# Second expert tile: who compares the keys and who weighs the one-hots of the scatter

## The chip, the cores and the metric

One core of a Trainium2 chip runs the kernel. Its engines are named TensorE (PE, with its weight loads as PEld), VectorE (DVE), ScalarE (ACT), GpSimd (POOL) and SyncE (SP, which only issues transfers here). The metric is the device time of one launch in microseconds (us), the median of the runs; lower is better. Times in the trace are counted from the first instruction of one profiled execution.

## The reference, cut to what matters

The model has three parts that follow each other (a gated MLP with spatial mixing, stick-breaking attention, a convolution and mLSTM mixer). The change lies in the last one, a layer of 16384 experts (PEER) for 256 tokens with 2048 features:

```python
q = (xt @ wq).reshape(-1, 8, 2, 128)                     # 8 heads, two half queries
s = einsum('thpc,hpnc->thpn', q, keys)                   # 128 first and 128 second keys
sv, si = top_k(s, 16)                                    # then the best 16 of the 16 x 16 pairs
eid = first_key * 128 + second_key                       # 128 experts for each token
gate = softmax(top_s)
act = gelu(einsum('thkd,td->thk', take(u, eid), xt))     # 128 dot products for each token
out = einsum('thk,thkd->td', gate * act, take(v, eid))
```

So each token has 128 picks: an expert (a pair of a first and a second key) and a weight, `gate * gelu(dot product)`.

## The kernel before, in words

**Tokens and stages.** The 256 tokens are two tiles of 128 (tile 0 and tile 1), a token for each of the 128 partitions. The expert layer has three stages.

1. *Rows of u.* For each of 256 rows (`r`, 128 for each tile) an indirect transfer gathers one row of `u` for each token of the tile, 1 MB in all, into a ring of buffers. VectorE does the dot product of most rows (`dot_row`); for two slots of the ring GpSimd multiplies (`scale_row`) and ScalarE sums (`sum_row`). Between the rows VectorE chooses the experts of later head groups, ScalarE takes exponentials of the gates (`gate_exponent`, the last at row 182), and the scatter of tile 0 is done, one step about every four rows.
2. *Scatter.* The weights of a token are spread into a 128 x 128 table over its two keys: the table of a token is a product of two one-hot matrices, `onehot_b` (pick k has second key b) transposed times `onehot_a` (pick k has first key a, times the weight of pick k). One **step** does this for 4 tokens (`SCATTER`), so a tile has 32 steps (`SCATTERS`). Steps are counted 0 to 31 within tile 1 in this text. A step is: the one-hots are made on the vector engines, TensorE multiplies (4 products, `scatter`, L1124; in fp32 each is two weight loads and two matmuls in the trace, so 8 of each in a step), and ScalarE copies the 4 tables from PSUM into `wT` in SBUF (`store_one`, L1475).
3. *Values.* 128 chunks: each has the dense product of `wT` with a chunk of the first 1152 columns of `v` (transfers of 576 KB by SyncE, products L1149 and L1155), and two gathered rows of the other 896 columns, weighed by VectorE (`weigh`, L2279; gathers by GpSimd, L716). Then the last layer norm and the output.

**Buffers and order.** Every engine runs its own program in the order in which the code is written, and the engines meet at semaphores. The one-hots have 4 slots (`HOT_SLOTS`): whoever fills the slot of step m waits for `scattered` to show that TensorE is done with step m-4. TensorE writes the tables of a step to one of two halves of PSUM: step m waits in `w_stored` for the store of step m-2. Of the value stage, 4 gathers and 3 dense chunks have buffers of their own and are issued before the scatter of tile 1 (`V_EARLY`); the other buffers lie where the one-hots and the picks lie, so the remaining transfers wait for the scatter's last step (`pool.wait_ge(scattered, TOKENS // SCATTER + 2)`, and the same in `load_v`).

**Between the last row of u and the first step of tile 1.** ScalarE copies the keys of tile 1 out of PSUM (`picks_out("keys1")`, L1209), loads the table of Gelu (`warm_up(ACT.Gelu)`, L1230), takes the Gelu of the dot products (`pick_gelu(1)`, L1461). VectorE multiplies with the gates (`weights(1)`, L2213). TensorE turns the weights so that picks lie on partitions (unit `picks1`, L1110), ScalarE copies them into `picksT[:, 2, ...]`. The keys are in `picksT[:, 0]` (first) and `picksT[:, 1]` (second).

**The one-hots of tile 1 before the change.** VectorE compares both keys of the 4 tokens in one instruction (`plain_one_hots`, L2195, 128 x 1024 numbers). Then the plain one-hot of the first key is weighed in place: token 0 of the step by ScalarE (`weigh_one_hot`, L1485), tokens 1 to 3 by GpSimd (`weigh_one_hots`, L703, 128 x 384). TensorE waits for both. ScalarE's order is: weigh step m, store step m-2. In tile 0 (`static_one_hots`) VectorE makes both itself: L2180 compares the second keys (128 x 512), L2184 makes a weighed one-hot of one token (128 x 128) four times.

Of the kernel before, what the change touches and what calls it, by code (L numbers as in the profile page):

```python
# [74 lines left out]
SCATTER = 4  # L75
SCATTERS = P // SCATTER
HOT_SLOTS = 4
ACT_TOKENS = 1

RAW_SLOTS = 4  # L80
SPLIT_SLOTS = 4
# [11 lines left out]
CHOICE_STEPS = (0, 3, 5, 7, 9, 11, 14, 17, 21)  # L93
EXPONENT, FINISH = 5, 8
LAST_ROW = TILES * PICKS - 1


def row_slot(r):
# [112 lines left out]
def build(nc, x, norm_g, a_w_in, a_v_norm_g, a_w_s, a_b_s, a_w_out, b_w_in, b_w_out, final_g, ln_in_g_2, ln_in_b_2,  # L211
# [6 lines left out]
    with ctx:  # L218
# [202 lines left out]
        def sem(name):  # L421
            return ctx.enter_context(nc.semaphore(name))
# [63 lines left out]
        wgt_done = sem("wgt_done")  # L486
        onehot_done = sem("onehot_done")
        weighed_by_pool = sem("weighed_by_pool")
        weighed_by_act = sem("weighed_by_act")
        scattered = sem("scattered")  # L490
        w_stored = sem("w_stored")
        v_raw_landed = [sem(f"v_raw_landed{s}") for s in range(V_CHUNKS)]
# [112 lines left out]
        def _(pool):  # L605
# [90 lines left out]
            def weigh_one_hots():  # L696

                is_emptied(pool, "picks1")
                for m in range(SCATTERS, TILES * SCATTERS):
                    first, end = m * SCATTER + ACT_TOKENS, (m + 1) * SCATTER  # L700
                    cut = onehot_a[m % HOT_SLOTS][:, ACT_TOKENS:, :]
                    pool.wait_ge(onehot_done, m + 1)
                    nc.gpsimd.tensor_tensor(  # L703
                        cut, cut, picksT[:, 2, first:end].unsqueeze(2).to_broadcast([P, SCATTER - ACT_TOKENS, N_KEYS]),
                        ALU.mult).then_inc(weighed_by_pool, 1)

            pool.wait_ge(keys_known, TILES)
            for t in range(TILES):
# [25 lines left out]
        def _(pe):  # L734
# [378 lines left out]
            def scatter(t):  # L1113

                for m in range(t * SCATTERS, (t + 1) * SCATTERS):
                    if t:
                        pe.wait_ge(weighed_by_pool, m - SCATTERS + 1)
                        pe.wait_ge(weighed_by_act, m - SCATTERS + 1)
                    else:
                        pe.wait_ge(onehot_done, m + 1)  # L1120
                    pe.wait_ge(w_stored, m + 1)
                    s = m % HOT_SLOTS
                    for n in range(SCATTER):
                        last = mm(by_128[B][:, m % 2 * SCATTER + n, :], onehot_b[s][:, n, :], onehot_a[s][:, n, :],  # L1124
                                  start=True, stop=True)
                    last.then_inc(scattered, 1)
# [48 lines left out]
        def _(act):  # L1175
# [300 lines left out]
                   by_128[B][:, s * SCATTER:(s + 1) * SCATTER, :].rearrange("p n a -> p a n"), ACT.Copy)\  # L1476
                    .then_inc(w_stored, 1)

            def weigh_one_hot(m):

                act.wait_ge(onehot_done, m + 1)
                for n in range(ACT_TOKENS):
                    token = m * SCATTER + n
                    cut = onehot_a[m % HOT_SLOTS][:, n, :]
                    ins = fn(cut, cut, ACT.Copy, scale=picksT[:, 2, token:token + 1])  # L1485
                ins.then_inc(weighed_by_act, 1)

            act.sem_inc(w_stored, 2)

            for n in range(CHOSEN_BEFORE):  # L1490
# [1 line left out]
            for r in range(TILES * PICKS):  # L1492
                if r == PICKS:
                    pick_gelu(0)
                    weigh_h(0)
                if r == PICKS + 5:
                    picks_out("picks0", picksT[:, :, 0:P], 3)
                if r + 1 == TILES * PICKS:
                    warm_up(ACT.Gelu)
                if by_pool(r):  # L1500
                    sum_row(r)
                for n in range(CHOSEN_BEFORE, ALL_GROUPS):
                    if r == CHOICE_ROW[n] + CHOICE_STEPS[EXPONENT] + 1:
                        gate_exponent(n)
                if r == PICKS - 4:
                    act.wait_ge(gates_done, CHOSEN_EARLY + 1)
                    fn(flat[A], h[:, 1, :], ACT.Copy).then_inc(h_copied, 1)
                for m in range(SCATTERS):
                    if r == one_hot_row(m) + 2:
                        store_one(0, m, m % 2)  # L1510
                if r == one_hot_row(SCATTERS - 1) + 2:
                    picks_out("keys1", picksT[:, 0:2, P:], 2)
            pick_gelu(1)
            picks_out("picks1", picksT[:, 2:3, P:], 1)
            is_emptied(act, "picks1")
            for m in range(SCATTERS + 2):
                if m < SCATTERS:
                    weigh_one_hot(SCATTERS + m)
                if m >= 2:
                    store_one(1, m - 2, m % 2)  # L1520
                if m == 2:
                    weigh_h(1)

            def round_chunk(c):
# [29 lines left out]
        def _(dve):  # L1554
# [632 lines left out]
                                                 op0=ALU.is_equal, op1=ALU.mult)  # L2187
                ins.then_inc(onehot_done, 1)

            def plain_one_hots(m):  # L2190

                wide = [P, 2, SCATTER, N_KEYS]
                token = m * SCATTER
                dve.wait_ge(scattered, m - 1)
                v.tensor_tensor(onehots[:, m % HOT_SLOTS, :, :, :],  # L2195
                                near_keys[1].unsqueeze(1).unsqueeze(1).to_broadcast(wide),
                                picksT[:, 0:2, token:token + SCATTER].unsqueeze(3).to_broadcast(wide), ALU.is_equal)\
                    .then_inc(onehot_done, 1)

            def dot_row(r):  # L2200

# [66 lines left out]
                        static_one_hots(m)  # L2268
            weights(1)
            is_emptied(dve, "keys1")  # L2270

            def weigh(r):

# [9 lines left out]
            def subtract_chunk(c):  # L2283
# [6 lines left out]
                v.tensor_tensor(v_split[u][:, 1, :], v_raw[c % V_CHUNKS][:, 0:V_SPLIT],  # L2290
                                v_split[u][:, 0, :].bitcast(F32), ALU.subtract).then_inc(v_lo, 1)

            for m in range(SCATTERS, TILES * SCATTERS):
                plain_one_hots(m)

            dve.wait_ge(h_weighed, TILES)
            def kept_stats(t):
# [61 lines left out]
```

## Time and profile before

| | |
|---|---|
| runs | 2971.75 us median of 3 (2969.94 to 2973.08) |
| profiled execution: span from first to last instruction | 2967.1 us, 28922 instructions |
| the rest of a run's time around that span (median less span) | 4.6 us |
| PE / DVE / ACT / POOL busy | 78% / 69% / 38% / 28% |
| mean granted TensorE clock | 0.884 of full speed |
| rows of u, both tiles | about 1760 to 2426 us |
| scatter of tile 1 | about 2426 to 2466 us |
| values | about 2466 to 2948 us, then the norm and output to 2967 |

The span is what the trace shows; the time of a run is a little longer since it holds what lies around the instructions. The granted clock of 1.0 is TensorE's level of 2.4 GHz, and 0.5 is that of 1.2 GHz. A row that is merged (x27) gives the time from the first start to the last end.

### The profile page before, as it was taken

Reading aid. Unit: us, or ns where it says so; the run is one execution under the profiler, and the core shown is the slowest. Engines: PE = TensorE matmul, PEld = TensorE weight load, DVE = VectorE, ACT = ScalarE, POOL = GpSimd, SP = SyncE. Lnnn points to the kernel's source line nnn. Section 1 sums busy time; section 2 is a strip of 40 time slices with the busy share of each in tenths; the row PEclk is TensorE's granted clock in tenths of the full one; section 3 lists DMA queues with packets and bytes.
Section 4 is the critical chain, followed back from the end, with each engine's and each line's share of the span. In section 5 each row is a group of like instructions: output and inputs, shape, how many; then the busy total and the mean of one; then the engine's idle time right before and its main releaser. Section 6 shows DMA issues by size and latency. Waiting matters only on the chain.

```text
span 2967.1 us, 28922 instructions
## 1 busy us (share of the span) xinstructions
PE 2323.2 (78%) x10371; PEld 1832.5 (62%) x10371; DVE 2035.6 (69%) x2513; ACT 1129.5 (38%) x1263; POOL 818.3 (28%) x646
## 2 busy tenths in 40 slices
PE   8999999999999999899999990000022249998997
PEld 7888888888888888688888770000011136555654
DVE  5456555554544555745665678999899888887888
ACT  5444344444444554444344442121222244222222
POOL 1000000000000000000000017888787875545553
PEclk9999999999999999999999995555555569999998
DMA  8666556666666546465566569999999977999997
GB/s 281 208 186 193 168 178 191 183 193 190 183 189 184 156 140 207 146 183 177 163 185 227 162 209 395 420 420 418 415 406 400 421 287 291 408 407 390 408 408 301
DMA packets 165303, 792.12 MB, mean 267 GB/s; under 512 B 20188, under 2 KB 20240, under 8 KB 131248
## 3 DMA queue, kind: packets, MB, share of 16 engines
q1 hardware_dynamic: 105344, 390.12, 41.1%
q0 software_dynamic: 59824, 400.23, 33.3%
q8 instruction: 82, 1.34, 0.2%
q14 instruction: 53, 0.43, 0.0%
HBM read 788.17 MB, written 2.10 MB: 266 GB/s over the span
## 4 chain that ended last, share of the span: by engine, by line
PE 57%; DVE 19%; DMA 13%; issue 6%; POOL 3%; ACT 1%; POOLq 0%; DVEq 0%; ACTq 0%
PE banks L749 52%; DMA v_rows<-in_peer_v_rest,eid 11%; DVE ring L2205 9%; DVE banks L2279 3%; DMA ring<-in_peer_u,eid 2%; POOL ring L674 2%; PE banks L781 1%; PE banks L1124 1%; POOL v_rows L716 1%; DVE onehots L2184 1%; DVE v_split L2290 1%; PE banks L761 1%; DVE w_split L1565 0%; DVE cand L2108 0%; PE banks L829 0%
## 5 line engine op out<-in xcount | busy, mean ns | idle before, releaser
L749 PE MATMUL banks<-w_split,xT 128*128 128x512 f32 x7008 | 1611.8, 391 | 8.5 <-DVE xT L1612 5.3
L749 PEld LDWEIGHTS banks<-w_split,xT 128*128 128x128 f32 x7008 | 1314.3, 188 | 282.5 <-DVE xT L1612 6.9
L1565 DVE TENSOR_TENSOR w_split<-w_raw,w_split 128x1024 fp32r<-128x1024 f32 x592 | 722.3, 1225 | 730.6 <-ACT w_split L1187 729.5
L1187 ACT ACTIVATE w_split<-w_raw 128x1024 fp32r<-128x1024 f32 x592 | 626.2, 1059 | 911.6 <-PE banks L749 875.4
L2205 DVE CUSTOM_DVE_ANT_0 ring<-ring,banks 128x2048 f32<-128x2048 f32 x194 | 438.5, 2285 | 46.3 <-DMA ring<-in_peer_u,eid 42.4
L2279 DVE SCALAR_TENSOR_TENSOR banks<-v_rows,wgt,banks 128x896 f32<-128x896 f32 x254 | 293.2, 1154 | 67.6 <-DMA v_rows<-in_peer_v_rest,eid 66.4
L674 POOL DMA_INDIRECT ring<-in_peer_u,eid x256 | 244.8, 956 | 258.4 <-DVE eid L2137 157.8
L716 POOL DMA_INDIRECT v_rows<-in_peer_v_rest,eid x256 | 245.3, 958 | 233.6 <-DVE banks L2279 202.0
L1155 PE MATMUL banks<-v_raw,wT 128*128 128x512 f32 (+1 forms) x1024 | 298.0, 434 | 0.7 <-ACT wT L1475 0.7
L609 POOL DMA_DIRECT2D row_a<-in_final_g x1 | 0.5, 534 | 1067.3 <-DVE ao L1827 1067.3
L1124 PE MATMUL banks<-onehots 128*128 128x128 f32 x512 | 103.0, 367 | 243.7 <-DVE onehots L2184 232.4
L683 POOL TENSOR_TENSOR ring<-ring,h 128x2048 f32<-128x2048 f32 x62 | 280.2, 4520 | 37.7 <-DMA ring<-in_peer_u,eid 36.2
L1448 ACT ACTIVATE ring<-ring 128x2048 f32<-128x2048 f32 x62 | 118.4, 1910 | 403.5 <-POOL ring L683 403.5
L1155 PEld LDWEIGHTS banks<-v_raw,wT 128*128 128x128 f32 x1024 | 174.2, 190 | 134.9 <-issue 123.0
L1110 PE MATMUL banks<-ident,pick_keys 128*128 128x128 f32 x4 | 1.3, 426 | 325.0 <-DVE wgt L2213 325.0
L1124 PEld LDWEIGHTS banks<-onehots 128*128 128x128 f32 x512 | 89.6, 265 | 257.3 <-DVE onehots L2184 241.6
L1149 PE MATMUL banks<-v_split,w_x 128*128 128x512 f32 x768 | 224.5, 423 | 9.6 <-DVE w_x L2287 9.6
L1110 PEld LDWEIGHTS banks<-ident,pick_keys 128*128 128x128 f32 x4 | 0.7, 218 | 325.2 <-issue 325.2
L1149 PEld LDWEIGHTS banks<-v_split,w_x 128*128 128x128 f32 x768 | 122.9, 190 | 58.9 <-DVE v_split L2290 25.0
L1529 ACT ACTIVATE w_x<-wT 128x256 fp32r<-128x256 f32 x128 | 53.2, 416 | 271.4 <-PE banks L1149 271.3
L1531 ACT ACTIVATE v_split<-v_raw 128x512 fp32r<-128x512 f32 x128 | 80.5, 629 | 66.6 <-DMA v_raw<-in_peer_v_dense 65.0
L609 POOL DMA_DIRECT2D row_a<-in_ln_g x1 | 0.5, 528 | 338.4 <-DVE xT L1612 338.4
(321 smaller groups left out, 1320.9 us busy)
## 6 DMA issues: line engine op xcount, KB each, us to landing
w_raw<-in_a_w_in SPq DMA_DIRECT2D x192, 512.0 KB, 3.5
v_raw<-in_peer_v_dense SPq DMA_DIRECT2D x128, 576.0 KB, 8.0
w_raw<-in_b_w_in SPq DMA_DIRECT2D x128, 512.0 KB, 3.5
w_raw<-in_w_in SPq DMA_DIRECT2D x112, 512.0 KB, 3.6
w_raw<-in_a_w_out SPq DMA_DIRECT2D x64, 512.0 KB, 4.5
w_raw<-in_b_w_out SPq DMA_DIRECT2D x32, 512.0 KB, 4.5
w_raw<-in_w_out SPq DMA_DIRECT2D x32, 512.0 KB, 4.4
w_raw<-in_peer_wq SPq DMA_DIRECT2D x32, 512.0 KB, 3.7
```

The lines of the kernel that those rows point to most:

```text
L674: nc.gpsimd.indirect_dma_start(out=ring[s][:, :], out_offset=None, in_=peer_u_2[0], in_offset=bass.IndirectOffsetOnAxis(ap=eid[:, r:r + 1] ...
L683: nc.gpsimd.tensor_tensor(ring[s][:, :], ring[s][:, :], h[:, r // PICKS, :], ALU.mult)\
L716: nc.gpsimd.indirect_dma_start(out=v_rows[r % V_SLOTS][:, :], out_offset=None, in_=peer_v_rest[0], in_offset=bass.IndirectOffsetOnAxis(ap= ...
L749: last = mm(ps[half][:, 2 * t + n, :], xt[:, xp, kk, tok], w_split[:, s, wp, n * BANK:(n + 1) * BANK], start=(k == 0 and xp == 0 and wp == ...
L1124: last = mm(by_128[B][:, m % 2 * SCATTER + n, :], onehot_b[s][:, n, :], onehot_a[s][:, n, :], start=True, stop=True)
L1149: return mm(v_banks[t][0], w_x[u][:, wp, 1 - t, :], v_split[u][:, vp, :], start=first and wp + vp == 0, stop=last and vp == 1)
L1155: mm(v_banks[t][1 + n][:, 0:width], wT[:, 1 - t, c, :], v_raw[s][:, lo:lo + width], start=first, stop=last)
L1187: fn(w_split[:, k % SPLIT_SLOTS, 0, :], w_raw[:, k % RAW_SLOTS, :], ACT.Copy).then_inc(hi_done, 1)
L1448: fn(ring[s][:, :], ring[s][:, :], ACT.Copy, accum_out=wgt[:, r:r + 1]).then_inc(rows_summed, 1)
L1565: v.tensor_tensor(w_split[:, s, 1, :], w_raw[:, k % RAW_SLOTS, :], w_split[:, s, 0, :].bitcast(F32), ALU.subtract).then_inc(split_done, 1)
L2205: v.tensor_tensor_reduce(out=ring[s][:, :], in0=ring[s][:, :], in1=flat[1 - r // PICKS], scale=1.0, scalar=0.0, op0=ALU.mult, op1=ALU.add, ...
L2279: v.scalar_tensor_tensor(out=v_sum, in0=v_rows[r % V_SLOTS][:, :], scalar=wgt[:, r:r + 1], in1=v_sum if m else h[:, t, V_DENSE:], op0=ALU. ...
```

## The change

The one-hots of tile 1 are made in another way. VectorE compares only the second keys (`key_one_hots`, 128 x 512) and makes the weighed one-hot of token 0 (`weighed_one_hots`, 128 x 128). GpSimd makes the weighed one-hots of tokens 1 to 3 from the keys and weights itself, with one `tensor_scalar` each (compare `iota_keys` with the first key, times the weight); it no longer waits for VectorE but for a free slot. ScalarE only stores. TensorE waits for `onehot_done` (VectorE) and `weighed_by_pool` (GpSimd). The second-key one-hots of steps 0 and 1 (`HOT_AHEAD`) are made before the weights are turned. The Gelu table of tile 1 is loaded at row index 183, behind the last exponential, and no longer at row 255.

```diff
-ACT_TOKENS = 1
+DVE_TOKENS = 1
+HOT_AHEAD = 2
+LAST_EXPONENT = CHOICE_ROW[ALL_GROUPS - 1] + CHOICE_STEPS[EXPONENT]
@@ GpSimd
                 is_emptied(pool, "picks1")
+                is_emptied(pool, "keys1")
                 for m in range(SCATTERS, TILES * SCATTERS):
-                    first, end = m * SCATTER + ACT_TOKENS, (m + 1) * SCATTER
-                    cut = onehot_a[m % HOT_SLOTS][:, ACT_TOKENS:, :]
-                    pool.wait_ge(onehot_done, m + 1)
-                    nc.gpsimd.tensor_tensor(
-                        cut, cut, picksT[:, 2, first:end].unsqueeze(2).to_broadcast([P, SCATTER - ACT_TOKENS, N_KEYS]),
-                        ALU.mult).then_inc(weighed_by_pool, 1)
+                    pool.wait_ge(scattered, m - 1)
+                    for n in range(DVE_TOKENS, SCATTER):
+                        token = m * SCATTER + n
+                        ins = nc.gpsimd.tensor_scalar(onehot_a[m % HOT_SLOTS][:, n, :], iota_keys[:, :],
+                                                      picksT[:, 0, token:token + 1], picksT[:, 2, token:token + 1],
+                                                      ALU.is_equal, ALU.mult)
+                    ins.then_inc(weighed_by_pool, 1)
@@ TensorE
                     if t:
                         pe.wait_ge(weighed_by_pool, m - SCATTERS + 1)
-                        pe.wait_ge(weighed_by_act, m - SCATTERS + 1)
-                    else:
-                        pe.wait_ge(onehot_done, m + 1)
+                    pe.wait_ge(onehot_done, m + 1)
@@ ScalarE
-                if r + 1 == TILES * PICKS:
+                if r == LAST_EXPONENT + 2:
                     warm_up(ACT.Gelu)
...
-            for m in range(SCATTERS + 2):
-                if m < SCATTERS:
-                    weigh_one_hot(SCATTERS + m)
-                if m >= 2:
-                    store_one(1, m - 2, m % 2)
-                if m == 2:
+            for m in range(SCATTERS):
+                store_one(1, m, m % 2)
+                if m == 0:
                     weigh_h(1)
@@ VectorE
-            def plain_one_hots(m):
...
+            def key_one_hots(m):
+
                 dve.wait_ge(scattered, m - 1)
...
+                return v.tensor_tensor(onehot_b[m % HOT_SLOTS], near_keys[1].unsqueeze(1).to_broadcast([P, SCATTER, N_KEYS]),
+                                       picksT[:, 1, m * SCATTER:(m + 1) * SCATTER].unsqueeze(2)
+                                       .to_broadcast([P, SCATTER, N_KEYS]), ALU.is_equal)
+
+            def weighed_one_hots(m):
+
+                for n in range(DVE_TOKENS):
+                    token = m * SCATTER + n
+                    ins = v.scalar_tensor_tensor(out=onehot_a[m % HOT_SLOTS][:, n, :], in0=near_keys[1],
+                                                 scalar=picksT[:, 0, token:token + 1],
+                                                 in1=picksT[:, 2, token:token + 1].to_broadcast([P, N_KEYS]),
+                                                 op0=ALU.is_equal, op1=ALU.mult)
+                return ins
@@
             is_emptied(dve, "keys1")
+            for m in range(SCATTERS, SCATTERS + HOT_AHEAD):
+                key_one_hots(m)
...
+            is_emptied(dve, "picks1")
             for m in range(SCATTERS, TILES * SCATTERS):
-                plain_one_hots(m)
+                if m >= SCATTERS + HOT_AHEAD:
+                    key_one_hots(m)
+                weighed_one_hots(m).then_inc(onehot_done, 1)
```

ScalarE's order before, from the copy of tile 1's keys on (`half_free` and `half_filled` are the semaphores of the PSUM halves, `h` the residual rows that are scaled for the value stage):

```order
L1209 ACTIVATE picksT<-banks 128x2x128 [waits half_filled_b]
L1230 ACT_TABLE_LOAD
L1230 ACTIVATE warm<-ident 128x1
L1461 ACTIVATE wgt<-wgt 128x128 [waits rows_summed,rows_used]
L1209 ACTIVATE picksT<-banks 128x128 [waits half_filled_a]
L1485 ACTIVATE onehots<-onehots,picksT 128x128 [waits onehot_done,half_free_a]
L1485 ACTIVATE onehots<-onehots,picksT 128x128 [waits onehot_done] x2
L1475 ACTIVATE wT<-banks 128x128x4 [waits scattered]
L1465 ACTIVATE h<-h 128x896
L1485 ACTIVATE onehots<-onehots,picksT 128x128 [waits onehot_done]
L1475 ACTIVATE wT<-banks 128x128x4 [waits scattered]
```

And now at the same place:

```order
L1210 ACTIVATE picksT<-banks 128x2x128 [waits half_filled_b]
L1462 ACTIVATE wgt<-wgt 128x128 [waits rows_summed,rows_used]
L1210 ACTIVATE picksT<-banks 128x128 [waits half_filled_a]
L1476 ACTIVATE wT<-banks 128x128x4 [waits scattered,half_free_a]
L1466 ACTIVATE h<-h 128x896
L1476 ACTIVATE wT<-banks 128x128x4 [waits scattered] x31
```

The table load and its warm-up have gone from here, and so have the weighings between the stores. The load now stands in the rows of u of tile 1, behind the last exponential (`gate`):

```order
L1449 ACTIVATE ring_154,wgt<-ring_154 128x2048 [waits rows_scaled]
L1455 ACTIVATE gate<-gate 128x32 [waits gate_sub]
L1476 ACTIVATE wT<-banks 128x128x4 [waits scattered]
L1231 ACT_TABLE_LOAD
L1231 ACTIVATE warm<-ident 128x1
L1449 ACTIVATE ring_158,wgt<-ring_158 128x2048 [waits rows_scaled]
```

It lies between a store of tile 0 and the next sum of a row. GpSimd's order before, from its last row of u (`ring`) on:

```order
L683 TENSOR_TENSOR ring_154<-ring_154,h 128x2048 [waits row_landed3]
L716 DMA v_rows_170<-in_peer_v_rest,eid 128x896 [waits keys_known,v_used]
L716 DMA v_rows_171<-in_peer_v_rest,eid 128x896 [waits v_used]
L716 DMA v_rows_172<-in_peer_v_rest,eid 128x896 [waits v_used]
L716 DMA v_rows_173<-in_peer_v_rest,eid 128x896 [waits v_used]
L703 TENSOR_TENSOR onehots<-onehots,picksT 128x384 [waits onehot_done,half_free_a]
L703 TENSOR_TENSOR onehots<-onehots,picksT 128x384 [waits onehot_done] x31
```

And now, from the fourth gather of the value stage on:

```order
L719 DMA v_rows_173<-in_peer_v_rest,eid 128x896 [waits v_used]
L705 TENSOR_SCALAR onehots<-iota_keys,picksT 128x128 [waits scattered,half_free_b,half_free_a]
L705 TENSOR_SCALAR onehots<-iota_keys,picksT 128x128 x2
L705 TENSOR_SCALAR onehots<-iota_keys,picksT 128x128 [waits scattered]
L705 TENSOR_SCALAR onehots<-iota_keys,picksT 128x128 x2
```

One instruction of 128 x 384 a step has become three of 128 x 128, and the wait is for the slot. VectorE now, from its last dot product (`ISA`) on:

```order
L2201 ISA wgt 128x1
L2209 TENSOR_TENSOR wgt<-wgt,gate 128x128 [waits gelu_done]
L2182 TENSOR_TENSOR onehots<-banks,picksT 128x512 [waits scattered,half_free_b,wgt_done]
L2182 TENSOR_TENSOR onehots<-banks,picksT 128x512 [waits scattered]
L2190 SCALAR_TENSOR_TENSOR onehots<-banks,picksT 128x128 [waits half_free_a]
L2190 SCALAR_TENSOR_TENSOR onehots<-banks,picksT 128x128
L2182 TENSOR_TENSOR onehots<-banks,picksT 128x512 [waits scattered]
L2190 SCALAR_TENSOR_TENSOR onehots<-banks,picksT 128x128
```

Where 32 comparisons of 128 x 1024 stood (L2195), two comparisons of 128 x 512 come ahead of the weights, and then one comparison and one weighed one-hot alternate.

## Rows read from the trace of the kernel before

**Rows 1.** Windows: busy us (and instructions) of each engine, TensorE's clock, DMA share, GB/s.
```profile
core 0: us, PE busy (x) PEld busy (x) DVE busy (x) ACT busy (x) POOL busy (x), PEclk, DMA share, GB/s
2168.00:2405.00 237.00, 51.90 (x200) 44.53 (x200) 218.25 (x334) 59.86 (x72) 191.38 (x116) 0.50 1.00 413
2426.00:2466.00 40.00, 37.09 (x257) 32.76 (x257) 36.69 (x33) 29.89 (x68) 27.07 (x33) 0.91 0.09 32
2480.00:2600.00 120.00, 120.00 (x460) 73.29 (x459) 101.43 (x130) 34.54 (x66) 61.69 (x65) 1.00 1.02 408
```

**Rows 2.** Chain of waits into the scatter: start, length, engine, tile, line.
```profile
2424.13 0.37 ACT picksT L1209
2424.52 1.28 ACT L1230
2426.02 0.21 ACT wgt L1461
2426.25 0.30 DVE wgt L2213
2426.58 1.24 DVE onehots L2195
2427.95 0.84 POOL onehots L703
2428.83 11.77 PE banks L1124 x80
```

**Rows 3.** Timeline (start, length, engine, line, ..., idle before): VectorE, GpSimd, ScalarE around the start.
```profile
2424.30 0.08 DVE L2205 DVE_READ_ACCUMULATOR2_ANT wgt<- 128x1 f32 x1
2425.67 0.95 POOL L716 DMA_INDIRECT v_rows<-in_peer_v_rest,eid  x1 [0.30 <-issue]
2427.11 0.28 ACT L1209 ACTIVATE picksT<-banks 128x128 f32<-128x128 f32 x1 [0.89 <-PE banks L1110]
2432.65 30.65 DVE L2195 TENSOR_TENSOR onehots<-banks,picksT 128x1024 f32<-128x1024 f32 x27 [0.32 <-PE banks L1124]
```

**Rows 4.** Timeline: stores of steps 2 to 5 and 31, last step's weight loads.
```profile
2433.79 0.60 ACT L1475 ACTIVATE wT<-banks 128x512 f32<-128x512 f32 x1 [0.25 <-PE banks L1124]
2434.68 0.60 ACT L1475 ACTIVATE wT<-banks 128x512 f32<-128x512 f32 x1
2435.70 0.60 ACT L1475 ACTIVATE wT<-banks 128x512 f32<-128x512 f32 x1
2436.59 0.60 ACT L1475 ACTIVATE wT<-banks 128x512 f32<-128x512 f32 x1
...
2464.33 0.97 PEld L1124 LDWEIGHTS banks<-onehots 128*128 128x128 f32 x8 [0.16 <-POOL onehots L703]
2465.53 0.60 ACT L1475 ACTIVATE wT<-banks 128x512 f32<-128x512 f32 x1 [0.54 <-PE banks L1124]
```

**Rows 5.** Windows of TensorE alone: length, busy (instructions), clock, DMA share.
```profile
2428.80:2433.00 4.20, 4.17 (x19) 0.50 0.23 96
2434.00:2438.00 4.00, 4.00 (x36) 1.00 0.02 4
```

**Rows 6.** Timeline: one-hots of a step of tile 0 on VectorE, GpSimd beside it.
```profile
2406.95 0.69 DVE L2180 TENSOR_TENSOR onehots<-banks,picksT 128x512 f32<-128x512 f32 x1
2407.25 4.52 POOL L683 TENSOR_TENSOR ring<-ring,h 128x2048 f32<-128x2048 f32 x1 [0.58 <-DMA ring<-in_peer_u,eid]
2407.55 1.12 DVE L2184 SCALAR_TENSOR_TENSOR onehots<-banks,picksT 128x128 f32<-128x128 f32 x4
```

**Rows 7.** Groups of GpSimd by form: busy us, mean ns of one.
```profile
L703 POOL TENSOR_TENSOR onehots<-onehots,picksT 128x384 f32<-128x384 f32 x32 | 26.5, 827 | 11.1 <-DVE onehots L2195 11.1
L729 POOL TENSOR_TENSOR h<-h,row_g 128x1024 f32<-128x1024 f32 x1 | 2.4, 2350 | 14.0 <-ACT h L1550 14.0
L616 POOL TENSOR_SCALAR_AFFINE_SELECT upto<-upto 128x128 f32<-128x128 f32 x1 | 0.3, 292 | 0.1
L615 POOL MEMSET upto<- 128x128 f32 x1 | 0.2, 196 | 0.0
```

**Rows 8.** Timeline: ScalarE behind the last exponential of the gates.
```profile
2243.06 0.60 ACT L1475 ACTIVATE wT<-banks 128x512 f32<-128x512 f32 x1 [1.58 <-PE banks L1124]
2246.80 1.91 ACT L1448 ACTIVATE ring<-ring 128x2048 f32<-128x2048 f32 x1 [3.14 <-POOL ring L683]
```

More of the change, by code:

```diff
@@ L488, in build @@
         weighed_by_pool = sem("weighed_by_pool")
-        weighed_by_act = sem("weighed_by_act")
         scattered = sem("scattered")
@@ L1477, in store_one @@
                     .then_inc(w_stored, 1)
[L1479 to L1486, printed above, removed]
             act.sem_inc(w_stored, 2)
@@ L2188, in static_one_hots @@
                 ins.then_inc(onehot_done, 1)
-            def plain_one_hots(m):
-                wide = [P, 2, SCATTER, N_KEYS]
-                token = m * SCATTER
+            def key_one_hots(m):
                 dve.wait_ge(scattered, m - 1)
[L2195 to L2198, printed above, removed]
+                return v.tensor_tensor(onehot_b[m % HOT_SLOTS], near_keys[1].unsqueeze(1).to_broadcast([P, SCATTER, N_KEYS]),
[9 more added lines that the diff above has]
+                return ins
             def dot_row(r):
```

## The prediction

> **What bounds the kernel now.** I read the windows by stage first [rows 1], then the chain of waits through the scatter of tile 1 [rows 2], then the timeline around its start and inside it [rows 3 to 5].
>
> The windows show three stages. While rows of u are gathered, the DMA share is 1.00 at 413 GB/s; in the value stage it is 1.02 at 408 GB/s. Between them lie 40 us, 2426 to 2466, with a DMA share of 0.09 [rows 1]. That hole is the scatter of tile 1: nearly every further transfer needs buffers that the scatter gives back at its end. The value stage is set by transfers, and these start when the last step is done. So I take every microsecond that the scatter ends sooner as one microsecond of the kernel, and nothing that happens to VectorE, GpSimd or ScalarE inside the hole matters otherwise.
>
> Inside the hole VectorE runs 27 comparisons of 128x1024 in 30.65 us without a gap, 1.135 us each, while TensorE waits 0.16 us for GpSimd in each late step [rows 3, 4]. TensorE is busy on paper (37.1 of 40 us), but it waits for one-hots: the bound of the steady part is VectorE's comparison.
>
> Which wait is next if the one-hots come faster? Here the early steps tell. The first ones pile up because TensorE runs at clock 0.50 (1.2 GHz) from 2428.8 to 2433.0, 19 instructions in 4.2 us, and has one-hots waiting when the clock is at 1.00 (2.4 GHz), where it starts about 35 in 4 us [rows 5]. (The granted clock rose 4.2 us after the products began.) In that stretch the stores of steps 2, 4 and of steps 3, 5 stand 1.91 us apart: 2433.79 and 2435.70, 2434.68 and 2436.59 [rows 4]. That is a loop through the two halves of PSUM. Step m may start when step m-2 is stored; from the start of its weight loads to its store are 1.20 us (2464.33 to 2465.53), the store takes 0.60, and the remaining 0.11 is the way from the store's end back to TensorE. 1.20 + 0.60 + 0.11 = 1.91 us for two steps, **0.955 us a step**. ScalarE's weighing is not in the loop as long as it ends before the step is ready to store. TensorE's own rate would be a little quicker than this loop: 8 instructions at 4.0/35 us are 0.91 us.
>
> **The change part by part.** The profiled execution has a span of 2967.1 us; 4.6 us lie around it in the median run of 2971.75. I work out differences in the profiled execution and take them off the median.
>
> *VectorE.* Instead of 1.135 us a step it has one 128x512 comparison and one weighed one-hot. In tile 0 the comparison starts 0.60 us before the next instruction, and four weighed one-hots of 0.34 take 1.12, so one starts each 0.26 us [rows 6]. 0.60 + 0.26 = 0.86 us a step, below 0.955. They keep these durations in tile 0 while GpSimd runs a 4.52 us multiplication beside them [rows 6], so I charge nothing for GpSimd now running at the same time. Two comparisons (1.2 us) are made ahead, while the weights are turned. VectorE is no bound any more.
>
> *ScalarE.* It loses the weighing and keeps 0.60 a step. Free.
>
> *GpSimd.* This is the unknown: three `tensor_scalar` of 128x128 with two scalars from memory; the trace has no such instruction. Bounds from the nearest rows: a memset of 128x128, which reads nothing, takes 0.196 us; a row that reads one tensor and selects by a comparison (affine select, 128x128) takes 0.292 [rows 7]. From above: two-input multiplications take 2.350 us for 1024 and 4.52 for 2048 columns, 2.12 ns a column with 0.18 us to begin with [rows 6, 7], which makes 0.45 us for 128. So a step costs GpSimd 3 x 0.196 = 0.59 to 3 x 0.45 = 1.35 us. I take the affine select, since it too has one input and one output and more than one operation per element, and add a little for the scalars: 0.30 each, **0.90 us a step**, below 0.955. That the same work on 384 columns with two inputs is 0.827 supports it. GpSimd also starts early enough: it can run up to four steps ahead and TensorE loses time to the clock in the first steps.
>
> The Trainium skill has a rule against this choice, in the page GPSIMD Engine Reference, section 7 (performance pitfalls for Q7 kernels): each small read command costs about 102 cycles that do not overlap with the one before. If each of the two scalars were such a read, that would be 0.17 us more at the 1.2 GHz which the page gives, an estimate of 0.46 us an instruction, 1.39 us a step. No row here shows it; the third rival below is what would happen then.
>
> *The start.* Now: the copy of the keys ends at 2424.50, then table load 1.28 and warm-up 0.2, Gelu from 2425.93, weights 2426.25 to 2426.55, turned, copied 2427.11 to 2427.39; VectorE compares from 2426.58 and GpSimd weighs 2427.95 to 2428.79; TensorE starts at 2428.83 [rows 2, 3]. Without the load the Gelu can start when VectorE's last dot product is in, 2424.38, so at 2424.45, 1.5 us earlier; the weights are in `picksT` at 2425.9. VectorE is done with step 0 by 2425.0 + 1.2 + 0.3 = 2426.6. GpSimd, however, is issuing its four gathers of v until 2426.62 [rows 3], which stand ahead of its one-hots. So it starts at 2426.65 and is done with step 0 0.9 us later: TensorE starts at **2427.55 instead of 2428.83, 1.28 us** sooner. Of the 1.5 us of the table load only about 0.8 can be used (without the load moved, GpSimd would start at 2427.45), the rest of the 1.28 is the comparison that GpSimd no longer waits for.
>
> *The table load at row 183.* ScalarE is idle 3.14 us there: the store ends at 2243.66, the next sum starts at 2246.80 [rows 8]. 1.28 + 0.20 fit in. What follows on ScalarE until the Gelu are copies. Cost 0; if the cover were missing, up to 1.5 us for a ring slot that comes free later.
>
> *The steps.* TensorE's step 4 began at 2434.39 + 0.11 = 2434.50, 5.67 us after its start; I keep these 5.67 (clock 0.50 for 4.2 us, then the loop). Step 31 began at 2464.33 [rows 4]: 27 steps in 29.83 us. By the loop they take 27 x 0.955 = 25.78. **4.05 us.** The last step and the store behind it stay the same.
>
> Sum: 1.28 + 4.05 = 5.3 us. GpSimd's limit, checked: its step 31 would be ready at 2426.65 + 32 x 0.90 = 2455.5, TensorE comes to that step at 2427.55 + 5.67 + 25.78 = 2459.0. So an instruction of GpSimd may take up to about (2459.0 - 2426.65)/96 = 0.337 us before it costs anything. Predicted: 2971.75 - 5.3 = **2966.4 us**.
>
> **The rivals.**
> (1) *The loop is not what limits.* If the 1.91 us were ScalarE's order of weighing and storing (0.40 + 0.60 is 1.0 a step, near the 0.955), TensorE would run by itself at about 0.90, the steps would gain 1.4 more: 6.7 in all, 2965.0. Against: the store of step 2 had 0.25 us of idle before it, released by TensorE. An earlier rise of the clock would give as much: each us at 1.00 instead of 0.50 spares about 0.45 us.
> (2) *GpSimd becomes the bound, mildly.* At 0.337 to 0.39 us an instruction the stage ends with GpSimd: at 0.37, step 31 ready at 2426.65 + 96 x 0.37 = 2462.2 instead of the 2464.25 of now; gain 2.1, 2969.7. For it: reading two scalars a time and three starts instead of one. Against: the affine select's 0.292.
> (3) *GpSimd is slower than the comparison it replaced.* The price of three short instructions against one long one; the place is `weighed_by_pool` in front of every product; it decides from (2464.25 - 2426.65)/96 = 0.392 us. At the upper bound of 0.45 step 31 is ready at 2469.9, 5.6 later than now: 2977.4. VectorE and ScalarE would then idle beside it.
> (4) *The gain doesn't reach the end*, because the value stage is bound elsewhere than by transfers. DMA share 1.02 speaks against it. 2971.
>
> **How the numbers follow.** Forecast (the loop, gain 4.5 to 5.9) 0.45; rival 1 0.17; rival 2 0.17; rival 3 0.16; rival 4 0.05. What a measurement can tell from no change is 0.2%, 5.9 us, and the forecast lies just inside of it: 2965.8 is the border. With about 1 us of scatter in a median, the forecast gives faster with 0.38, rival 1 with 0.85, none of the others: 0.17 + 0.14, and some 0.02 for a GpSimd or a clock better than I allow: 0.33. Slower by over 5.9 us needs 0.453 us an instruction, the far end of rival 3: 0.06. Same 0.61. The range goes from 2964.3 (rival 1 with scatter) up to 2973.5 (rival 3 up to 0.41 us an instruction); the forecast's own is 2965.2 to 2967.6.
>
> **What would show it.** In the changed profile: the GpSimd group of `tensor_scalar`, 96 of them, at about 0.30 us (the number on which all hangs); stores of the second tile 0.95 to 0.96 us apart from step 4 on, each second pair 1.91; TensorE's first product at 2427.5; Gelu at 2424.5; the last store 5.3 us earlier; DMA share 1.0 from there and the end as many us earlier; ScalarE's table load in a gap near 2244. Stores 0.90 apart speak for rival 1, a TensorE that waits for `onehots` of GpSimd in each step for rival 2 or 3. The prediction is wrong in its mechanism if the one-hots of VectorE get longer beside GpSimd, or if the value stage takes longer than the 482 us from 2466 to 2948.

## The result, and the profile after

The changed kernel takes 3010.6 us (median of 4, 3006.03 to 3013.05) against 2971.28 us before (4 runs): ratio 1.0127, 95% interval 1.0115 to 1.0139. It is 39.3 us slower; 5.3 us faster was forecast. The profiled execution has a span of 3011.3 us, 44.2 more than the 2967.1 of before; 4.4 of them arise before the scatter (the last dot product ends at 2428.80, before at 2424.38 [rows 3]), as executions differ by some microseconds here.

The group of new GpSimd instructions settles the matter (trace after, instructions that write or read `onehots`, ns min/median/max):

```profile
L705 POOL TENSOR_SCALAR onehots<-iota_keys,picksT x96: 780/781/810, 2431.1 to 2504.6; 128x128 f32<-128x128 f32 x96
L2182 DVE TENSOR_TENSOR onehots<-banks,picksT x32: 675/690/692, 2429.5 to 2497.3; 128x512 f32<-128x512 f32 x32
L2190 DVE SCALAR_TENSOR_TENSOR onehots<-banks,picksT x32: 336/340/343, 2430.7 to 2498.0; 128x128 f32<-128x128 f32 x32
```

0.781 us instead of the 0.30 that I took, and instead of at most 0.45. VectorE's two instructions are as predicted. The chain of waits after, from the gathers of v to the first value products (start, length, engine, tile, line):

```profile
2430.09 0.95 POOL v_rows L719
2431.04 0.05 issue
2431.09 74.30 POOL onehots L705 x96
2505.39 0.04 issue
2505.43 2.09 PE banks L1125 x8
2507.52 0.02 issue
2507.55 0.60 ACT wT L1476
2508.15 0.04 issue
2508.20 4.63 PE banks L1156 x8
```

Where seven kinds of work alternated before [rows 2], one engine's queue is the whole scatter: 96 instructions in 74.30 us, 0.774 from start to start, 2.32 us a step. The waits say the same from the other side (engine line <- who; us, times, longest):

```profile
ACT wT L1476 <- PE banks L1125: 57.9, 32, 5.4
DVE onehots L2182 <- PE banks L1125: 38.7, 28, 2.6
PEld banks L1125 <- POOL onehots L705: 31.2, 32, 3.8
```

All others wait. Windows of before's kind (busy us and instructions of each engine, clock, DMA share, GB/s), the scatter and the value stage:

```profile
2430.00:2508.00 78.00, 54.17 (x257) 46.35 (x256) 29.59 (x64) 20.08 (x34) 75.23 (x97) 0.70 0.05 18
2524.00:2644.00 120.00, 120.00 (x465) 75.48 (x464) 101.00 (x129) 34.32 (x66) 61.86 (x64) 1.00 1.02 408
```

The hole in the transfers is now 78 us wide at a DMA share of 0.05, and the value stage has the same share and rate as before [rows 1]. TensorE, waiting in every step, has a mean clock of 0.70 there, before 0.91. From the end of the last dot product to the start of the last store it is 2507.55 - 2428.80 = 78.75 us, before 2465.53 - 2424.38 = 41.15 [rows 3, 4]: **37.6 of the 39.3 us**. Inside these 37.6 us the chain is longer by more than GpSimd's 96 instructions: from the last step's weight loads to its store are 2.12 us here (2505.43 to 2507.55) and 1.20 before [rows 4], with TensorE's granted clock at 0.50 in that stretch here and at 1.00 before. The other 1.7 us I don't attribute: the span's rest behind the start of the last store is 503.8 us after and 501.6 before, but 502.8 in experiment 5, whose scatter is like that of before, so executions differ by more than a microsecond there.

The Gelu, the start of GpSimd's one-hots and the table load came as described, the first product did not (timeline after):

```profile
2428.72 0.08 DVE L2201 DVE_READ_ACCUMULATOR2_ANT wgt<- 128x1 f32 x1
2428.84 0.31 ACT L1462 ACTIVATE wgt<-wgt 128x128 f32<-128x128 f32 x1
2430.09 0.95 POOL L719 DMA_INDIRECT v_rows<-in_peer_v_rest,eid  x1 [0.30 <-issue]
2431.09 11.65 POOL L705 TENSOR_SCALAR onehots<-iota_keys,picksT 128x128 f32<-128x128 f32 x15
2433.51 1.78 PEld L1125 LDWEIGHTS banks<-onehots 128*128 128x128 f32 x8 [3.80 <-POOL onehots L705]
...
2248.18 1.28 ACT L1231 ACT_TABLE_LOAD   x1
2249.47 0.20 ACT L1231 ACTIVATE warm<-ident 128x1 f32<-128x1 f32 x1
2251.29 1.91 ACT L1449 ACTIVATE ring<-ring 128x2048 f32<-128x2048 f32 x1 [1.61 <-POOL ring L684]
```

The Gelu starts 0.04 us after the last dot product's end (before 1.6 us after it), GpSimd begins the one-hots right behind its fourth gather, and the load stands in a gap that has 1.61 us left. But step 0 needs three of GpSimd's instructions, so TensorE's first weight load comes 4.71 us after the last dot product (2433.51 - 2428.80), 0.26 later than before's 4.45 and not 1.28 sooner.

### The profile page after: what moved, and what is told of

It is laid out like the page before. It is cut to its first block, busy times and chain, and to the rows that moved or that the text cites. A ratio compares the mean times of both kernels' runs of the same rounds, so it can differ in the third digit from the quotient of the medians.

```text
span 3011.3 us, 28986 instructions
## 1 busy us (share of the span) xinstructions
PE 2347.1 (78%) x10371; PEld 1853.0 (62%) x10371; DVE 2030.5 (67%) x2545; ACT 1119.1 (37%) x1231; POOL 869.0 (29%) x710
## 4 chain that ended last, share of the span: by engine, by line
PE 57%; DVE 18%; DMA 13%; issue 6%; POOL 5%; ACT 1%; POOLq 0%; SPq 0%; DVEq 0%; ACTq 0%
PE banks L752 51%; DMA v_rows<-in_peer_v_rest,eid 10%; DVE ring L2201 9%; DMA ring<-in_peer_u,eid 3%; POOL onehots L705 2%; DVE banks L2277 2%; POOL ring L675 2%; PE banks L784 1%; POOL v_rows L719 1%; PE banks L1156 1%; DVE onehots L2173 1%; DMA v_raw<-in_peer_v_dense 1%; PE banks L764 1%; DVE cand L2097 0%; DVE w_split L1554 0%
## 5 line engine op out<-in xcount | busy, mean ns | idle before, releaser
L1125 PE MATMUL banks<-onehots 128*128 128x128 f32 x512 | 120.6, 409 | 266.0 <-DVE onehots L2173 233.2
L1125 PEld LDWEIGHTS banks<-onehots 128*128 128x128 f32 x512 | 103.4, 300 | 283.3 <-DVE onehots L2173 242.4
```

## The experiments

The theory after the result: one GpSimd `tensor_scalar` of 128 x 128 costs 0.774 us, and all that was lost is 32 steps of three of them. A GpSimd that waits for free slots is no rival: in the chain above the 96 follow each other without a gap. What is open is what in the instruction costs so much, and whether the rest of the prediction (the loop of TensorE and ScalarE, the start) would have held. Experiments 1 to 3, 7, 10 and 11 change only the instruction itself, so that their one-hots are not the right ones; they are read for the time of one instruction from start to start, which is the length of 96 in the timeline, divided by 96. Each of them was run once; on the chips that they ran on, one run of the kernel before took 2976.63 us beside experiments 1 to 4, and 2969.28 us beside 10 and 11.

### 1 to 3: numbers for scalars, half the width, one operation

```diff
 e1_numbers, changed kernel with:
-    picksT[:, 0, token:token + 1], picksT[:, 2, token:token + 1], ALU.is_equal, ALU.mult)
+    5.0, 2.0, ALU.is_equal, ALU.mult)
 e2_half_width, changed kernel with:
-    ins = nc.gpsimd.tensor_scalar(onehot_a[m % HOT_SLOTS][:, n, :], iota_keys[:, :],
+    ins = nc.gpsimd.tensor_scalar(onehot_a[m % HOT_SLOTS][:, n, 0:64], iota_keys[:, 0:64],
 e3_one_op, changed kernel with:
-    picksT[:, 0, token:token + 1], picksT[:, 2, token:token + 1], ALU.is_equal, ALU.mult)
+    picksT[:, 0, token:token + 1], None, ALU.is_equal)
```

> GpSimd's 96 one-hot instructions of tile 1 take numbers in the instruction (5.0 and 2.0) in place of the two scalars per partition, so the weighed one-hots of tokens 1 to 3 are not those of the picks. The changed kernel has 0.774 us from start to start (74.30 us for 96). Theory A (the two scalars are reads that don't overlap): about 0.30 to 0.35 us each, the affine select's 0.292 and a little, the stage 96 x 0.44 = 42 us shorter until TensorE's loop binds, about 2968 us. Theory B (each column is slow in this instruction whatever the scalars are): 0.77 stays, and about 3010 us. Theory C (a fixed price for a tensor_scalar instruction on GpSimd): 0.77 stays as well; the half width tells B from C.

> The 96 instructions write only the first 64 columns of each one-hot (the rest keeps what lay there), with both scalars. Theory A (scalar reads): 0.774 less 64 columns at about 0.9 to 1.7 ns, 0.66 to 0.72 us. Theory B (about 6 ns a column): about 0.40 us. Theory C (fixed price): 0.66 to 0.72 us as in A.

> The 96 instructions only compare (one scalar, no multiplication), so tokens 1 to 3 are not weighed. Theory A (scalar reads, half of the extra each): about 0.55 us. Theory B with a price for each operation and column: between 0.4 and 0.6 us. If the comparison itself is the slow operation: 0.70 or more. Theory C (fixed): 0.74 or more.

Measured, one line of the timeline of each (start, length of all 96):

```profile
2429.86 68.00 POOL L705 TENSOR_SCALAR onehots<-iota_keys 128x128 f32<-128x128 f32 x96
```

```profile
2428.06 53.48 POOL L705 TENSOR_SCALAR onehots<-iota_keys,picksT 128x64 f32<-128x64 f32 x96
```

```profile
2430.99 55.67 POOL L705 TENSOR_SCALAR onehots<-iota_keys,picksT 128x128 f32<-128x128 f32 x96
```

0.708 us with numbers (one run, 3002.95 us), 0.557 at half width (2988.03), 0.58 with the comparison alone (2991.17). Theory A falls: the two scalars from memory cost 0.066 us a start together (0.774 - 0.708), not 0.45. The recorded length of one instruction fell by more, from 781 to 641 ns, but then GpSimd idled before the next one, 6.5 us in all where it had idled 0.1 (groups of the changed kernel and of experiment 1: busy us, mean ns of one, idle us before):

```profile
L705 POOL TENSOR_SCALAR onehots<-iota_keys,picksT 128x128 f32<-128x128 f32 x96 | 74.3, 781 | 0.1
L705 POOL TENSOR_SCALAR onehots<-iota_keys 128x128 f32<-128x128 f32 x96 | 61.6, 641 | 6.5
```

The Trainium skill, GPSIMD Engine Reference, section 7, has about 102 cycles for each small read, by which two would cost an estimated 0.17 us. The 0.14 us of recorded length is not far from that, the 0.066 us from start to start is well under it, and no run here tells whether such reads are what was spared. Either way it is a small part of 0.774 us.

Theory C falls too, since half of the columns takes away 0.22 us. What is left is B in kind, a price by width and by operations, but not with the figures that I gave it: with numbers 0.77 should have stayed, and half the width should have come to 0.40, not 0.557. There is also a part that doesn't depend on the width, which the next three measure.

### 7, 10, 11: another operation, a quarter of the width, multiplication alone

```diff
 e7_subtract:            ALU.is_equal, ALU.mult  ->  ALU.subtract, ALU.mult
 e10_quarter_width:      [..., n, :], iota_keys[:, :]  ->  [..., n, 0:32], iota_keys[:, 0:32]
 e11_multiply_only:      picksT[:, 2, token:token + 1], None, ALU.mult
```

> The 96 instructions of GpSimd subtract the scalar in place of comparing with it, then multiply: tokens 1 to 3 get no one-hots. So far: 128 columns with both scalars 0.773, with numbers in the instruction 0.709, 64 columns 0.556, comparison alone 0.579. Theory B1 (any operation costs about 1.5 to 2 ns a column): 0.77 stays. Theory B2 (the comparison, which makes a truth value and then a number, is the slow one): 0.45 to 0.60.

> The 96 instructions of GpSimd write 32 columns of each one-hot with both scalars (the rest keeps what lay there). From 0.773 at 128 and 0.556 at 64 columns, a straight line is 3.4 ns a column with 0.34 us to begin with: 0.447 us at 32. If there is a step (a fixed price for a long instruction): 0.55 as at 64. The step of TensorE would be 3 x 0.447 = 1.34 us.

> The 96 instructions of GpSimd only multiply the counted keys by the weight (one scalar, no comparison), so tokens 1 to 3 get no one-hots. Comparison alone took 0.579. If each operation has the same price: 0.58. If the comparison is the dearer one: less, down to about 0.40.

```profile
2430.97 74.42 POOL onehots L705 x96
```

```profile
2427.85 43.23 POOL L705 TENSOR_SCALAR onehots<-iota_keys,picksT 128x32 f32<-128x32 f32 x96
```

```profile
2432.65 55.77 POOL L705 TENSOR_SCALAR onehots<-iota_keys,picksT 128x128 f32<-128x128 f32 x96
```

The first line is from the chain of waits, the others from the timeline. Subtraction costs what the comparison costs (0.775), and multiplying alone costs what comparing alone costs (0.58): among these three, the kind of operation doesn't matter. 32 columns take 0.45, 64 take 0.557, 128 take 0.774: a straight line of **3.4 ns a column for the two operations, with 0.34 us to begin with**. A single operation with one scalar saves 0.194 us of the 0.774; it takes away an operation and a scalar at once, and since it ran at one width only, how the 0.194 divides into a part by column and a fixed part isn't shown. Times: 3011.56, 2975.33 and 2994.36 us, one run each.

### 4: the loop behind it

```diff
 e4_one_of_three, changed kernel with:
-    for n in range(DVE_TOKENS, SCATTER):
+    for n in range(DVE_TOKENS, DVE_TOKENS + 1):     # GpSimd's one-hots of tokens 2 and 3 are not made
```

> GpSimd makes only the one-hot of token 1 in each step; those of tokens 2 and 3 are left as they lie. GpSimd then needs 0.774 us a step, less than the 0.955 of the loop over the two halves of PSUM. If that loop is the next bound as predicted: stores of steps 4 to 31 0.955 us apart (1.91 for two), TensorE's first product about 1.1 to 1.2 us after the last gather's issue ends, the scatter about 5.3 us shorter than in the kernel before and the time about 2966 us. Rival 1 of the prediction (TensorE's own rate): 0.90 us apart, about 2965 us. If VectorE's two instructions with their waits are more than the 0.86 taken: stores more than 0.97 us apart with TensorE waiting for VectorE.

The last dot product and the stores in its timeline, steps 3 to 7 and the last:

```profile
2424.97 0.08 DVE L2201 DVE_READ_ACCUMULATOR2_ANT wgt<- 128x1 f32 x1
...
2434.67 0.60 ACT L1476 ACTIVATE wT<-banks 128x512 f32<-128x512 f32 x1 [0.33 <-PE banks L1125]
2435.65 0.60 ACT L1476 ACTIVATE wT<-banks 128x512 f32<-128x512 f32 x1 [0.38 <-PE banks L1125]
2436.58 0.60 ACT L1476 ACTIVATE wT<-banks 128x512 f32<-128x512 f32 x1 [0.33 <-PE banks L1125]
2437.56 0.60 ACT L1476 ACTIVATE wT<-banks 128x512 f32<-128x512 f32 x1 [0.38 <-PE banks L1125]
2438.49 0.60 ACT L1476 ACTIVATE wT<-banks 128x512 f32<-128x512 f32 x1 [0.33 <-PE banks L1125]
...
2461.38 0.60 ACT L1476 ACTIVATE wT<-banks 128x512 f32<-128x512 f32 x1 [0.33 <-PE banks L1125]
```

Every second store 1.91 us apart to the end, and from 2438.49 to 2461.38 it is 22.89 us for 24 steps: 0.954. ScalarE has nothing but stores here and still idles 0.33 to 0.38 before each, so it was not ScalarE's order, and rival 1 falls. VectorE and GpSimd are ahead of TensorE (GpSimd is busy for 20.66 of 27.60 us, and VectorE starts a comparison each 0.92 to 0.98 us where 0.86 would do), so the one-hots are not the bound either. The loop stands by its period and because the others are ruled out; no run changed the halves of PSUM themselves. TensorE's first weight load is at 2428.22, 3.17 us after the last dot product's end at 2425.05; before it was 4.45. From the dot product to the last store: 36.33 us, 4.8 less than before's 41.15. Of the forecast 5.3, the start gave 1.28, and the steps 3.5 instead of 4.05, with the clock at 0.50 until at least 5.2 us after the first product here, not 4.2. All of the missing part lies in the first steps: the store of step 4 starts 7.43 us after the first product (2435.65 - 2428.22), before 6.87 (2435.70 - 2428.83 [rows 2, 4]), while from there to the last store it is 25.73 us, where 25.78 was forecast.

Windows of it, as in [rows 1]:

```profile
2428.22:2433.40 5.18, 5.18 (x24) 5.18 (x25) 2.94 (x7) 2.03 (x3) 3.85 (x5) 0.50 0.39 138
2433.40:2461.00 27.60, 27.60 (x233) 27.43 (x233) 24.42 (x52) 17.27 (x29) 20.66 (x26) 1.00 0.01 1
```

Its one run took 2964.71 us, beside 2976.63 for one of the kernel before on the same chip; single runs differ by several microseconds, so the 36.33 is the figure to trust.

### 8 and 9: more one-hots on VectorE, the full computation

```diff
 e8_dve_two:    DVE_TOKENS = 1  ->  2
 e9_dve_three:  DVE_TOKENS = 1  ->  3
```

> The changed kernel with DVE_TOKENS = 2: VectorE makes two weighed one-hots a step, GpSimd two. If GpSimd's 0.774 us an instruction is the whole cause, steps are 2 x 0.774 = 1.55 us apart, 32 x 0.774 = 24.8 us less than the changed kernel: about 2986 us, 1.005 of the time before. If something of the step is fixed (a wait between the engines): less than 24.8 is regained. If GpSimd's instructions get quicker or slower with what VectorE does beside them: not 1.55.

> The changed kernel with DVE_TOKENS = 3: GpSimd makes one one-hot a step (0.774 us) and is no bound; VectorE has 0.60 + 3 x 0.26 = 1.38 us a step. Steps 1.38 us apart, 30 us less than the changed kernel: about 2980.5 us, 1.003 of the time before. If VectorE's weighed one-hot costs more than 0.26 beside GpSimd's instruction (both read the keys and weights), the steps are longer than 1.40.

Weight loads of three steps, timeline of the first and of the second:

```profile
2455.20 0.97 PEld L1125 LDWEIGHTS banks<-onehots 128*128 128x128 f32 x8 [0.58 <-POOL onehots L705]
2456.75 0.97 PEld L1125 LDWEIGHTS banks<-onehots 128*128 128x128 f32 x8 [0.58 <-POOL onehots L705]
2458.30 0.97 PEld L1125 LDWEIGHTS banks<-onehots 128*128 128x128 f32 x8 [0.58 <-POOL onehots L705]
```

```profile
2455.17 0.97 PEld L1125 LDWEIGHTS banks<-onehots 128*128 128x128 f32 x8 [0.40 <-issue]
2456.55 0.97 PEld L1125 LDWEIGHTS banks<-onehots 128*128 128x128 f32 x8 [0.41 <-issue]
2457.92 0.97 PEld L1125 LDWEIGHTS banks<-onehots 128*128 128x128 f32 x8 [0.40 <-issue]
```

Steps of 1.55 and 1.37 us, as the durations say (2 x 0.774 on GpSimd; 0.60 + 3 x 0.26 on VectorE). Medians of 2982.43 us (5 runs), ratio 1.0035 (1.0022 to 1.0049), and 2978.28 us (10 runs), ratio 1.0021 (1.0012 to 1.0030), against 2971.12 before. With two weighed one-hots on VectorE, so one GpSimd instruction less in each step, the way from the end of the last dot product to the start of the last store is 53.23 us, by two rows of the timeline of experiment 8:

```profile
2424.80 0.08 DVE L2201 DVE_READ_ACCUMULATOR2_ANT wgt<- 128x1 f32 x1
...
2478.11 0.60 ACT L1476 ACTIVATE wT<-banks 128x512 f32<-128x512 f32 x1 [0.95 <-PE banks L1125]
```

Its chain between them:

```profile
2427.18 49.69 POOL onehots L705 x64
2476.91 1.17 PE banks L1125 x8
```

That is 25.5 less than the changed kernel's 78.75, where 24.8 was foreseen: 24.6 of it are GpSimd's (74.30 - 49.69), and 0.9 the last step's products, which take 1.17 us here and 2.09 there. It is also 12.1 more than before's 41.15, where the medians differ by 11.3. The median is 28 us under the changed kernel's, 2.7 more than these 25.5; they come from other executions and I did not separate them. So as long as GpSimd is the bound, the damage goes by the number of its instructions; in experiment 9 VectorE's 1.37 us is the bound, still above the 1.135 us of before.

### 5: the Gelu table alone

```diff
 e5_gelu_alone, kernel before with:
-                if r + 1 == TILES * PICKS:
+                if r == LAST_EXPONENT + 2:
                     warm_up(ACT.Gelu)
```

> The kernel before with one edit, the Gelu table of tile 1 loaded at row index 183. Theory: the Gelu starts 1.4 to 1.5 us sooner after the last dot product, VectorE's first comparison and with it the first product (4.46 us after the last dot product before) come 1.3 us sooner (GpSimd is free of its gathers then), and since VectorE bounds all steps at 1.131 us the scatter ends 1.3 us sooner: about 0.9996 of the time before, not to be told from no change. Rival: the early load delays a sum of a row and so a slot of the ring, and the rows of u get 1 us or more longer: 0 or slower.

```profile
2251.06 1.91 ACT L1449 ACTIVATE ring<-ring 128x2048 f32<-128x2048 f32 x1 [1.62 <-POOL ring L684]
...
2430.55 0.08 DVE L2206 DVE_READ_ACCUMULATOR2_ANT wgt<- 128x1 f32 x1
...
2433.68 6.47 PEld L1125 LDWEIGHTS banks<-onehots 128*128 128x128 f32 x38 [2.14 <-POOL onehots L704]
...
2470.43 0.60 ACT L1476 ACTIVATE wT<-banks 128x512 f32<-128x512 f32 x1 [0.53 <-PE banks L1125]
```

From the last dot product's end (2430.63) the first weight load comes 3.05 us later instead of 4.45, the last store 39.80 instead of 41.15: the edit spares 1.35 us in place. In the times it doesn't show: 2972.14 us (11 runs) to 2971.12, ratio 1.0 (0.9991 to 1.0009). The interval of 0.9 per mille is 2.7 us wide on each side, so a gain of 1.35 can neither be confirmed nor excluded by it. The rival, a slot of the ring that comes free later, has no sign: the first sum of a row behind the load still waits 1.62 us for GpSimd (first row).

No kernel here beats the one before by more than can be measured while it computes everything.

## Why the prediction was wrong, point by point

**The view of the stages** held. The scatter is a hole in the transfers, and what it lengthens, the kernel lengthens: 37.6 of 39.3 us are in it, the value stage keeps its share and rate.

**The failed step** is the price of GpSimd's instruction: "I take the affine select" and "0.30 each, **0.90 us a step**". It measured 0.774, 2.32 us a step. What was lost follows from that number: by rival 3's border of 0.392 us, 96 x (0.774 - 0.392) = 36.7 us, and with the 0.9 us by which the last step is longer at the lower clock that makes the 37.6 us measured. Experiment 8 bears it out with another count: 64 instructions in 49.69 us, 0.776 each.

**The bounds** were wrong as well, and that is the worse fault. I called 0.45 us the upper end because a two-input instruction, by the slope between 1024 and 2048 columns, would come to that at 128. This took for granted that one input is cheaper than two, and that the straight line holds far below 1024 columns. Neither is borne out. The `tensor_scalar` with one input and two operations has 3.4 ns a column where `tensor_tensor` with two inputs and one operation had 2.12, and even with one operation it took 0.58 us at 128 columns. The line itself gives 0.18 + 384 x 0.00212 = 0.99 us for 384 columns, and the row for them has 0.827 [rows 7]. How much of the difference is the second operation and how much the other kind of instruction, no run separates. The two rows I held against each other, the affine select at 0.292 and the multiplication at 0.827 for 384 columns, were instructions of other kinds; neither tells of the two operations with scalars. The row that should have widened the range was the multiplication on 384 columns: 0.827 us was the one price in the trace for a GpSimd instruction of the one-hots, and no row ruled out that three instructions in its place would each cost nearly that, 3 x 0.827 = 2.48 us a step. That the outcome of 2.32 lies near it is chance, as that row has three times the columns and is of another kind. The "supports it" that I wrote of this row had no ground.

**Rival 3** named the mechanism, the place (`weighed_by_pool`) and, by the sum above, the border (0.392 us an instruction) rightly, and was given 0.16 and a price that was capped by the same false bound: 2977.4 instead of 3010.6.

**The rule of the Trainium skill** (GPSIMD Engine Reference, section 7) would have given an estimated 1.39 us a step. It spoke for the right side, but its price for two reads, 0.17 us, is small beside what was missing: without the scalars in memory an instruction still takes 0.708 us (experiment 1), not 0.30.

**VectorE beside GpSimd**: right. 0.69 and 0.34 as before, and GpSimd's 780 to 810 ns hold whether VectorE works or waits (it waits 38.7 us of that stage).

**The loop at 0.955 us**: right, borne out by experiment 4 with 0.954 over 24 steps. TensorE's own rate of 0.91 us, though, was counted in the very stretch in which the loop held it at 0.955, and instructions that only partly fall into that window make the count a little high, so those rows alone couldn't tell rival 1 from the forecast. **The start**: 1.28 us forecast, and 1.28 measured in experiment 4, but by luck: there one instruction takes the 0.8 to 0.9 us that I gave to three. In the changed kernel itself the first product came 0.26 us later than before. **The steps**: 4.05 forecast, 3.5 measured with GpSimd out of the way. The 0.56 us missing are in the steps before step 4, where the clock rose at least 1 us later; by the prediction's 0.45 us for each us of the lower clock that accounts for most of it, which is an estimate. **The table load at row 183**: right, no cost found and 1.35 us gained in place by itself.

**Two slips without effect on the sum.** VectorE's end of step 0, 2425.0 + 1.2 + 0.3, is 2426.5, not 2426.6. And the 4.6 us "around the span" are taken from two executions: where a run's time and its own span are both on record they differ by 1.7 (3013.05 and 3011.3), and the rest is the difference between executions.

## What to carry to other kernels

Before work is moved to GpSimd in an instruction that the trace doesn't hold, take its price as unknown upwards by a factor of two or more: here it was 2.6 (0.774 to 0.30), and neither fewer inputs nor a neighbour among its instructions bounded it. Write down first what duration of that one instruction turns the change around (here 0.392 us), and time one such instruction. And splitting one long instruction into three short ones multiplies the part that doesn't depend on the width: here 3 x 0.34 us a step, more by itself than the 0.955 us of the loop that was to be reached.

## What the runs showed of the hardware that was not expected

- GpSimd's `tensor_scalar` on fp32, 128 partitions: 0.450, 0.557 and 0.774 us from start to start at 32, 64 and 128 columns with two operations and two scalars from memory; 0.71 with two numbers in place of the scalars; 0.58 with one operation and one scalar, comparison or multiplication alike.
- VectorE makes the same weighed one-hot in 0.26 us, so GpSimd is 3 times slower in it; GpSimd's `tensor_tensor` for the multiplication of 384 columns took 0.827 us.
- TensorE's granted clock was at 0.50 for 4.2 us after the first product in one execution and for at least 5.2 in another, and its mean over the scatter fell from 0.91 to 0.70 when it waited in each step for GpSimd (0.54 to 1.35 us).
